# Ten of 31 convolution taps moved to ScalarE, the last block shared anew, means spread by a matrix of 1/D

## What is computed

```python
def conformer_conv_layer(x, norm_pre, w_pw1, b_pw1, w_dw, b_dw, ln_g, ln_b,
                         w_pw2, b_pw2, norm_post):
    h = rms_norm(x, norm_pre)
    p = jnp.einsum('bsd,de->bse', h, w_pw1) + b_pw1
    g = p[..., :D_C] * jax.nn.sigmoid(p[..., D_C:])
    conv = lax.conv_general_dilated(
        g, w_dw[:, None, :], window_strides=(1,), padding=[(CONV_K - 1, 0)],
        dimension_numbers=('NWC', 'WIO', 'NWC'), feature_group_count=D_C) + b_dw
    c = jax.nn.silu(layer_norm(conv, ln_g, ln_b))
    y = jnp.einsum('bse,ed->bsd', c, w_pw2) + b_pw2
    return x + rms_norm(y, norm_post)
```

## Time and profile before

| | before |
|---|---|
| median of 3 runs | 2025.27 us (2024.93 to 2025.52) |
| span of the profiled execution | 2021.2 us |
| TensorE busy | 1998.1 us (99%) |
| weight loads of TensorE busy | 1696.4 us (84%) |
| VectorE busy | 1189.4 us (59%) |
| ScalarE busy | 983.6 us (49%) |
| GpSimd busy | 199.5 us (10%) |

### The profile page before, as it was taken

One profiled execution on the slowest core, in us unless ns is written; L12 is line 12 of the kernel. 1 busy time (PEld: TensorE's weight loads), 2 busy tenths in 40 slices (PEclk: granted clock), 3 DMA queues, 4 the chain that ended last, 5 costly groups with the idle time before them and its releaser, 6 DMA issues.

```text
span 2021.2 us, 27616 instructions
## 1 busy us (share of the span) xinstructions
PE 1998.1 (99%) x9842; PEld 1696.4 (84%) x9842; DVE 1189.4 (59%) x1499; ACT 983.6 (49%) x1150; POOL 199.5 (10%) x123
## 2 busy tenths in 40 slices
PE   9999999999999999999999999999999999999998
PEld 7898888888888888888899977888888888888886
DVE  5755565555555554444799975655555555554444
ACT  6544464545455443433744464454444444443433
POOL 1000000000000000000689830000000000000000
PEclk9999999999999999999999989999999999999999
DMA  9745566766666765555355525566666666665554
GB/s 324 238 144 191 176 217 221 222 216 213 217 216 219 219 219 195 192 196 191 127 189 179 177 94 198 168 238 217 211 215 222 216 222 212 217 212 194 193 192 146
DMA packets 137966, 407.58 MB, mean 202 GB/s; under 512 B 15330, under 2 KB 38498, under 8 KB 137378
## 3 DMA queue, kind: packets, MB, share of 16 engines
q1 hardware_dynamic: 135796, 396.84, 59.6%
q0 software_dynamic: 2096, 9.70, 1.4%
HBM read 392.84 MB, written 13.63 MB: 201 GB/s over the span
## 4 chain that ended last, share of the span: by engine, by line
PE 88%; DVE 9%; ACT 1%; DMA 1%; issue 1%; SPq 0%; POOL 0%; DVEq 0%; ACTq 0%
PE acc L1297 83%; DVE acc L1211 7%; PE acc L1308 1%; PE acc L1310 1%; PE acc L1309 1%; PE acc L1538 1%; DMA raw<-in_units 1%; PE acc L1349 0%; ACT w_hi L570 0%; DVE gated L1198 0%; DVE conv L1216 0%; DVE conv L1211 0%; DVE w_lo L915 0%; DVE conv L1249 0%; PE acc L1347 0%
## 5 line engine op out<-in xcount | busy, mean ns | idle before, releaser
L917 DVE SCALAR_TENSOR_TENSOR w_lo<-raw,vecs,w_hi 128x1024 fp32r<-128x1024 f32 x398 | 509.2, 1282 | 437.3 <-ACT w_hi L570 437.1
L570 ACT ACTIVATE w_hi<-raw,vecs 128x1024 fp32r<-128x1024 f32 x398 | 457.8, 1152 | 514.2 <-PE acc L1297 471.9
L570 ACT ACTIVATE w_hi<-raw 128x1024 fp32r<-128x1024 f32 x304 | 321.2, 1059 | 397.2 <-PE acc L1297 352.3
L915 DVE TENSOR_TENSOR w_lo<-raw,w_hi 128x1024 fp32r<-128x1024 f32 x236 | 288.9, 1225 | 320.8 <-ACT w_hi L570 320.8
L1297 PE MATMUL acc<-w_hi,xT_hi 128*128 128x512 f32 x1528 | 472.0, 390 | 2.2 <-DVE w_lo L917 1.7
L1297 PE MATMUL acc<-w_lo,xT_hi 128*128 128x512 f32 x1528 | 470.5, 389 | 0.0
L1297 PE MATMUL acc<-w_hi,xT_lo 128*128 128x512 f32 x1528 | 470.5, 389 | 0.0
L1297 PEld LDWEIGHTS acc<-w_hi,xT_hi 128*128 128x128 f32 x1528 | 285.7, 188 | 63.7 <-issue 3.4
L1297 PEld LDWEIGHTS acc<-w_hi,xT_lo 128*128 128x128 f32 x1528 | 286.8, 188 | 59.8
L1297 PEld LDWEIGHTS acc<-w_lo,xT_hi 128*128 128x128 f32 x1528 | 286.8, 188 | 59.7
L1297 PE MATMUL acc<-w_lo,hT_hi 128*128 128x512 f32 x704 | 217.4, 389 | 0.0
(11 more groups left out here) (171 smaller groups left out, 1444.3 us busy)
## 6 DMA issues: line engine op xcount, KB each, us to landing
raw<-in_units SPq DMA_DIRECT2D x702, 512.0 KB, 3.8
hid_turned_blocks<-tok SPq DMA_DIRECT2D x44, 256.0 KB, 2.8
tok<-hid_turned_blocks SPq DMA_DIRECT2D x176, 64.0 KB, 2.8
gpost<-in_post POOLq DMA_DIRECT2D x4, 1024.0 KB, 6.0
x<-in_x POOLq DMA_DIRECT2D x4, 512.0 KB, 11.1
c_raw<-in_consts POOLq DMA_DIRECT2D x4, 512.0 KB, 7.3
out<-x SPq DMA_DIRECT2D x8, 256.0 KB, 2.8
xT_raw<-in_xT SPq DMA_DIRECT2D x3, 512.0 KB, 8.9
```

Source lines behind the costliest of these rows:

```text
L570: nc.scalar.activation(w_hi[:, s, :], raw[:, s, :], ACT.Copy, scale=scale).then_inc(hi_ready, 1)
L915: ins = nc.vector.tensor_tensor(w_lo[:, s, :], raw[:, s, :], w_hi[:, s, :], ALU.subtract)
L917: ins = nc.vector.scalar_tensor_tensor(w_lo[:, s, :], raw[:, s, :], vecs[:, gain:gain + 1], w_hi[:, s, :], ALU.mult, ALU.subtract)
```

## The change

- **Taps.** In blocks 0 to 14 ScalarE multiplies taps 21 to 30, two at a time side by side: the first pair into PSUM bank 6, four pairs into SBUF (`prod`). VectorE adds pair after pair 512 wide (`add_tap_pair`), does taps 2 to 20 as before, and adds the two halves of the sum of pairs. The closing add of a block moves behind the first tap of the next, the gate product behind tap 17; that of block 15 stands behind block 14.
- **Block 15.** VectorE takes taps 0 to 18; ScalarE multiplies 19 to 30, TensorE adds these twelve, and VectorE adds the three parts.
- **Means.** A 128 x 128 matrix of 1/D makes mean and spread in one matmul; most of the sums stand ahead of the products of block 15. Only the reciprocal root is still spread by a diagonal. `PE_WARM` goes from 8 to 6.
- **Bias.** Its split moves behind the third quad of the output projection, its memset to GpSimd, both `add_bias` stand inside the projection, each ahead of the fourth quad of its column half.
- **Order of splits.** GpSimd's split of the projection's first quad is interleaved with `add_pair`; ScalarE's last piece of it stands behind the products. The second quad is split two or three steps earlier.

The diff, with indentation cut, continued lines joined and removed lines that the listing above shows cut to the first:

```diff
-PE_WARM = 8
+PE_WARM = 6
+PAIRED = 5
+SINGLE = TAPS - 2 * PAIRED
+LAST_PE = 12
+LAST_DVE = TAPS - LAST_PE
...
-prod = mrow("prod", [P, 4, SEQ])
+prod = mrow("prod", [P, 2 * (PAIRED - 1), SEQ])
-diag = mrow("diag", [P, 2, SEQ])
+pair_sum = mrow("pair_sum", [P, 2 * SEQ])
+diag = mrow("diag", [P, SEQ])
+mean_of = mrow("mean_of", [P, P])
...
+nc.gpsimd.memset(mean_of[:], 1.0 / D).then_inc(consts_set, 1)
...
+split(Q_PW2, 0)
+split(Q_PW2, 1)
 add_pair(PAIRS - 1)
-for s in range(4):
-  split(Q_PW2, s)
+split(Q_PW2, 2)
+split(Q_PW2, 3)
 load_post(2)
+nc.gpsimd.memset(bias_rows[:].bitcast(F32), 0.0).then_inc(bias_cleared, 1)
 inv_root(cvar_ready, 1, crs[:], cvar[:, :, 1], crs_ready)
...
+def tap_pair(n, p):
+  for i in range(2):
+    j = SINGLE + 2 * p + i
+    if p == 0:
+      if n:
+        act.wait_ge(pair_added, (PAIRED - 1) * n)
+      dst = acc[:, 6, i * SEQ:(i + 1) * SEQ]
+    else:
+      if n:
+        act.wait_ge(pair_added, (PAIRED - 1) * (n - 1) + p)
+      dst = prod[:, 2 * (p - 1) + i, :]
+    last = nc.scalar.activation(dst, gated[:, n % RING, j:j + SEQ], ACT.Copy, scale=taps[:, n, j:j + 1])
+  last.then_inc(pair_ready, 1)
 nc.scalar.activation(warm[:], pow_exp[:], ACT.Sigmoid)
-split(Q_PW1 + 1, 0)
...
+for s in range(3):
+  split(Q_PW1 + 1, s)
 for n in range(LAST):
   gate(n)
   split(Q_PW1 + n + 1, 3)
-  if n < INIT_LATE:
-    begin_taps(n)
+  begin_taps(n)
+  tap_pair(n, 0)
   split(Q_PW1 + n + 2, 0)
-  if n >= INIT_LATE:
-    begin_taps(n)
+  tap_pair(n, 1)
+  tap_pair(n, 2)
   split(Q_PW1 + n + 2, 1)
+  tap_pair(n, 3)
+  tap_pair(n, 4)
   if n >= 3 and n % 2:
     square_pair((n - 3) // 2)
+  if n == LAST - 1:
+    square_pair(PAIRS - 1)
   split(Q_PW1 + n + 2, 2)
 gate(LAST)
-split(Q_PW2, 3)
...
 act.wait_ge(conv_ready, LAST)
 nc.scalar.activation(sq_last[:, 0, :], conv[:, LAST - 1, :], ACT.Square).then_inc(sq_last_ready, 1)
-act.wait_ge(prod_used, TAPS)
...
+slots = 2 * (PAIRED - 1)
+act.wait_ge(glu_ready, LAST + 1)
+for i in range(LAST_PE):
+  j = LAST_DVE + i
+  if i >= slots:
+    act.wait_ge(prod_used, i - slots + 1)
+  nc.scalar.activation(prod[:, i % slots, :], gated[:, LAST % RING, j:j + SEQ], ACT.Copy, scale=taps[:, LAST, j:j + 1]).then_inc(prod_ready, 1)
+split(Q_PW2, 3)
 act.wait_ge(conv_last_ready, 1)
 nc.scalar.activation(sq_last[:, 1, :], conv[:, LAST, :], ACT.Square).then_inc(sq_last_ready, 1)
...
-  if k >= KT // 2 and k % 2:
-    split(Q_PW2 + 1, k // 2 - KT // 4)
+  if 5 <= k <= 11 and k % 2:
+    split(Q_PW2 + 1, (k - 5) // 2)
 hi_c(KT - 1)
-for k in range(2, 5):
-  split_quad(Q_PW2 + k)
+split_quad(Q_PW2 + 2)
+split_bias()
+split_quad(Q_PW2 + 3)
+split_quad(Q_PW2 + 4)
...
-nc.vector.memset(bias_rows[:].bitcast(F32), 0.0).then_inc(bias_cleared, 1)
...
-def convolve(n, next_at):
...
+chain_at = {}
+def chain_step(n, half):
+  if (n, half) in chain_at:
+    dve.wait_ge(tap_done, chain_at[n, half])
+  else:
+    dve.wait_ge(taps_begun, 2 * n + 2)
+  chain_at[None] = chain_at.get(None, 0) + 1
+  chain_at[n, half] = chain_at[None]
+  return acc[:, 4 + n % 2, half * SEQ:(half + 1) * SEQ]
+def single_tap(n, j):
+  m = chain_step(n, j % 2)
+  out = conv[:, n, :] if j == SINGLE - 2 else m
+  nc.vector.scalar_tensor_tensor(out, gated[:, n % RING, j:j + SEQ], taps[:, n, j:j + 1], m, ALU.mult, ALU.add).then_inc(tap_done, 1)
+def add_tap_pair(n, p):
+  dve.wait_ge(pair_ready, PAIRED * n + p + 1)
+  if p > 1:
+    dve.wait_ge(pair_added, (PAIRED - 1) * n + p - 1)
+  out = pair_sum[:] if p == PAIRED - 1 else acc[:, 6, :]
+  nc.vector.tensor_tensor(out, acc[:, 6, :], prod[:, 2 * (p - 1):2 * p, :].rearrange("p i n -> p (i n)"), ALU.add).then_inc(pair_added, 1)
+def add_pair_sum(n, half):
+  dve.wait_ge(pair_added, (PAIRED - 1) * (n + 1))
+  m = chain_step(n, half)
+  nc.vector.tensor_tensor(m, m, pair_sum[:, half * SEQ:(half + 1) * SEQ], ALU.add).then_inc(tap_done, 1)
+def close_chain(n):
+  dve.wait_ge(tap_done, chain_at[n, 0])
+  dve.wait_ge(tap_done, chain_at[n, 1])
   nc.vector.tensor_tensor(conv[:, n, :], conv[:, n, :], acc[:, 4 + n % 2, 0:SEQ], ALU.add).then_inc(conv_ready, 1)
+def convolve(n):
+  single_tap(n, 2)
+  if n:
+    close_chain(n - 1)
+  for j in range(3, 13):
+    single_tap(n, j)
+  add_tap_pair(n, 1)
+  single_tap(n, 13)
+  single_tap(n, 14)
+  add_tap_pair(n, 2)
+  single_tap(n, 15)
+  single_tap(n, 16)
+  add_tap_pair(n, 3)
+  single_tap(n, 17)
+  if n < LAST - 1:
+    glu(n + 1)
+  single_tap(n, 18)
+  add_tap_pair(n, 4)
+  single_tap(n, 20)
+  add_pair_sum(n, 1)
+  add_pair_sum(n, 0)
+  single_tap(n, 19)
 glu(0)
 for n in range(LAST):
-  convolve(n, 8 if n == LAST - 1 else 26)
+  convolve(n)
+close_chain(LAST - 1)
+glu(LAST)
+def convolve_last():
+  g = gated[:, LAST % RING, :]
+  half = [acc[:, 5, i * SEQ:(i + 1) * SEQ] for i in range(2)]
+  dve.wait_ge(glu_ready, LAST + 1)
+  nc.vector.tensor_scalar(half[0], g[:, 0:SEQ], taps[:, LAST, 0:1], vecs[:, V_BDW + LAST:V_BDW + LAST + 1], ALU.mult, ALU.add).then_inc(last_tap_done, 1)
+  nc.vector.tensor_scalar(half[1], g[:, 1:1 + SEQ], taps[:, LAST, 1:2], None, ALU.mult).then_inc(last_tap_done, 1)
+  for j in range(2, LAST_DVE):
+    dve.wait_ge(last_tap_done, j - 1)
+    out = conv[:, LAST, :] if j == LAST_DVE - 2 else half[j % 2]
+    nc.vector.scalar_tensor_tensor(out, g[:, j:j + SEQ], taps[:, LAST, j:j + 1], half[j % 2], ALU.mult, ALU.add).then_inc(last_tap_done, 1)
+  dve.wait_ge(prods_summed, 1)
+  dve.wait_ge(last_tap_done, LAST_DVE - 1)
+  after(nc.vector.tensor_tensor(conv[:, LAST, :], conv[:, LAST, :], acc[:, 6, 0:SEQ], ALU.add))
+  dve.wait_ge(last_tap_done, LAST_DVE)
+  nc.vector.tensor_tensor(conv[:, LAST, :], conv[:, LAST, :], half[(LAST_DVE - 1) % 2], ALU.add).then_inc(conv_last_ready, 1)
+convolve_last()
...
-dve.wait_ge(sq_summed, 3)
...
+def centre(k):
+  nc.vector.tensor_tensor(conv[:, k, :], conv[:, k, :], acc[:, 4, 0:SEQ], ALU.subtract).then_inc(c_centred, 1)
+dve.wait_ge(means_ready, 1)
+after(nc.vector.tensor_copy(cvar[:, :, 0], acc[:, 4, SEQ:SEQ + T]))
+after(nc.vector.tensor_tensor(cvar[:, :, 0], cvar[:, :, 0], cvar[:, :, 0], ALU.mult))
+dve.wait_ge(squares_ready, 1)
+after(nc.vector.tensor_tensor(cvar[:, :, 1], acc[:, 7, 0:T], cvar[:, :, 0], ALU.subtract))
 nc.vector.tensor_scalar(cvar[:, :, 1], cvar[:, :, 1], 0.0, EPS, ALU.max, ALU.add).then_inc(cvar_ready, 1)
-for t in range(T):
...
+centre(0)
 dve.wait_ge(crs_ready, 1)
 for t in range(T):
-  last = nc.vector.tensor_scalar(diag[:, 1, t * P:(t + 1) * P], ident[:], crs[:, t:t + 1], None, ALU.mult)
...
+  last = nc.vector.tensor_scalar(diag[:, t * P:(t + 1) * P], ident[:], crs[:, t:t + 1], None, ALU.mult)
+last.then_inc(crs_diag_ready, 1)
 centre(1)
-dve.wait_ge(cst_spread, 2)
+dve.wait_ge(crs_spread, 1)
 for k in range(KT):
   dve.wait_ge(c_centred, k + 1)
-  nc.vector.tensor_tensor(conv[:, k, :], conv[:, k, :], acc[:, 4, 0:SEQ], ALU.mult).then_inc(c_normed, 1)
+  nc.vector.tensor_tensor(conv[:, k, :], conv[:, k, :], acc[:, 6, 0:SEQ], ALU.mult).then_inc(c_normed, 1)
   if k < KT - 2:
     centre(k + 2)
   if k > 1:
     lo_c(k - 2)
-  if k > KT // 2 and k % 2 == 0:
-    split(Q_PW2 + 1, k // 2 - KT // 4 - 1)
+  if 6 <= k <= 12 and k % 2 == 0:
+    split(Q_PW2 + 1, k // 2 - 3)
 lo_c(KT - 2)
 lo_c(KT - 1)
-split(Q_PW2 + 1, 3)
...
+split_quad(Q_PW2 + 2)
+dve.wait_ge(bias_hi_ready, 3)
+nc.vector.tensor_tensor(bias_rows[32:33, :], tok[32:33, :], bias_rows[32:33, :], ALU.subtract).then_inc(bias_lo_ready, 1)
+split_quad(Q_PW2 + 3)
+split_quad(Q_PW2 + 4)
...
-       start=True, stop=False)
+       start=False, stop=False)
...
+def sum_channels(out, src, first, stop):
+  for t in range(T):
+    last = mm(out[:, t:t + 1], src[:, t * P:(t + 1) * P], mean_of[:, 0:1], start=first and t == 0, stop=stop, skip_group_check=True)
   return last
+means, squares = acc[:, 4, SEQ:SEQ + T], acc[:, 7, 0:T]
+def average(src, first, stop):
+  mm(acc[:, 4, 0:SEQ], mean_of[:], src, start=first, stop=stop, skip_group_check=True)
+  return sum_channels(means, src, False, stop)
 pe.wait_ge(consts_set, 4)
 pe.wait_ge(sq_added, 2 * (PAIRS - 1))
 for b in range(2):
-  last = sum_channels(conv_sum[:, b, :], sq_sum[:, b, :], b == 0, False)
-last.then_inc(sq_summed, 1)
+  sum_channels(squares, sq_sum[:, b, :], b == 0, False)
 pe.wait_ge(conv_ready, LAST)
+for b in range(2):
+  average(conv_sum[:, b, :], b == 0, False)
+average(conv[:, LAST - 1, :], False, False)
+for i in range(LAST_PE):
+  pe.wait_ge(prod_ready, i + 1)
+  last = mm(acc[:, 6, 0:SEQ], ident[:], prod[:, i % (2 * (PAIRED - 1)), :], start=i == 0, stop=i == LAST_PE - 1)
+  if i < LAST_PE - 1:
+    last.then_inc(prod_used, 1)
+  else:
+    last.then_inc(prods_summed, 1)
 pe.wait_ge(sq_last_ready, 1)
-sum_channels(conv[:, LAST - 1, :], sq_last[:, 0, :], False, False).then_inc(sq_summed, 1)
+sum_channels(squares, sq_last[:, 0, :], False, False)
 pe.wait_ge(conv_last_ready, 1)
+average(conv[:, LAST, :], False, True).then_inc(means_ready, 1)
 pe.wait_ge(sq_last_ready, 2)
```

(12 more changed lines are left out.)

83 lines of the change are left out of this document (24 added, 59 removed).

## The result

| | before | after |
|---|---|---|
| median | 2025.39 us (2024.93 to 2026.16, 4 runs) | 2011.86 us (2010.40 to 2012.65, 4 runs) |
| span of the profiled execution | 2021.2 us | 2009.8 us |
| TensorE busy | 1998.1 us | 1988.8 us (99%) |
| ScalarE busy | 983.6 us | 1033.4 us (51%) |
| VectorE busy | 1189.4 us | 1182.1 us (59%) |

The ratio is 0.9932 with an interval of 0.9920 to 0.9944. Five more runs of the kernel after (experiment 4) gave 2011.07 (2010.24 to 2014.93). The forecast was 2013.1, range 2009.7 to 2018.

The account below looks back on a forecast made before the run. VectorE's debt of 0.70 us a convolution block, behind full TensorE, ends in a 31.9 us hole before dense work. Earlier start -12.0, split stall -1.3, bias +1.1: -12.2 from 2025.3 gives 2013.1 us, range 2009.7 to 2018.

Parts of the forecast that it names:

- No idle time at 998: First convolution block: moving the bias split removes TensorE's stall on a weight split, 1.57 us from start to start.
- VectorE's block: Convolution stage: VectorE's work per block falls from 12.2 to 11.27 us, 0.25 below TensorE's 11.52.
- rival 1: VectorE, not TensorE, ends the last block, as the clock returns early or never falls: 2011.7 us; chance 0.18.
- rival 2: VectorE still lags: its convolution block is 11.9 us, 0.35 too long, 14 times: 2016.6 us; chance 0.20.
- rival 3: Waits in ScalarE's queue hit the weight splits, TensorE idles 0.8 us a block: about 2025 us; chance 0.05.
- rival 4: VectorE's new adds hold up GpSimd, so TensorE waits 3.1 us a block: 2059 us; chance 0.05.
- the hole: Between the last convolution matmul and the next dense work: 21 to 22 us, where before it was 31.9.
- signs of being wrong: VectorE's block over 11.6; TensorE waiting for GpSimd; GpSimd's root over 0.5 us behind the variance; idle before a bias matmul.
- Term 1: Last block: TensorE's clock falls to half near 1169.3 for 3 to 6.5 us; its summed products are ready at 1180.3.
- Term 2: From last block ready, 1181.2, to dense work, 1188.3: norm steps, with 0.2 for late GpSimd and 0.3 for half clock.
- Term 3: Norm behind the last block: one of two spreads with its diagonal counted as removed from the path.
- Term 4: Whole kernel: -12.2 us, with 4.1 us kept between profiled span and median, gives 2013.1 us.

Follow-up runs that it names:

- experiment 4: Five more runs, on one chip, of the kernel after unchanged, 2011.07 us, and of it with ten matmuls of ones in the idle time, 2007.89 us.
- experiment 5: Kernel after with 8 of the last block's products on TensorE in place of 12, VectorE taking 23 taps: 2010.15 us.
- experiment 2: Kernel after with the bias split, its memset and VectorE's subtraction back in the first block: 2013.61 us.
- experiment 3: Kernel after plus ten matmuls of ones behind TensorE's last convolution matmul: 2007.83 us, ratio 0.9916.
- Experiment 9: Kernel of experiment 3 with the means summed into one column and spread by a diagonal as before: 2008.55 us.
- experiment 7: Kernel of experiment 3 with ScalarE's bias rows and VectorE's memset back in the first block, VectorE's subtraction left late: 2008.50 us.
- experiment 10: Kernel of experiment 3 with ScalarE's and VectorE's splits of the projection's second quad at their old, later places: 2008.68 us.
- experiment 1: Kernel before with only the pairs of taps from the change: 2021.05 us, ratio 0.9980.
- experiment 6: Kernel after with the sum of pairs in SBUF instead of PSUM, so wide adds read two SBUF tiles: 2062.8 us, ratio 1.0187.

## Why the prediction was right, and where its sizes were off

**Right, step by step.** No idle time at 998; last convolution matmul done at 1166.73 where 1166.77 was forecast. VectorE's block 11.31 of work against 11.27, so the lower ends of both bounds were the right ones, as wide adds start 0.60 apart. ScalarE 9.67 against 10.0: four products into SBUF take 1.70 us in its timeline, so they start 0.40 apart and not 0.455, eight times 0.055 less (0.44, of which 0.33 shows). The gate product of block 15 done at 1170.41 against 1170.5. VectorE waits for TensorE's products, as the forecast had it against rival 1, and experiment 5 shows that this wait sets the end. No idle time on a split behind it, and the bias inside the dense work costs its 1.13 us and no waiting (1221.96 to 1223.09 in the trace). Rivals 2, 3 and 4 fall with the profile: no lag, no small idle times, and GpSimd's splits at a median of 2.41 with none above 2.44. Of the signs named, one was missed narrowly: the hole, from the end of the last convolution matmul, was to be 21 to 22 us and was 22.35. None of the signs of being wrong appeared.

**Term 1, too small: the stretch at half clock.** I had products done at 1180.3 from a fall near 1169.3 that lasts 3 to 6.5 us. It came 2.4 us later, at 1171.7, and lasted 6.8, so all of it lay over averages and products: it cost 3.4 us, and they were done at 1181.5. The working itself was loose: a return of the clock at 1172.5 or 1175.7 costs 1.2 or 2.8 us from 1170.1 on, which gives 1179.1 to 1180.7 and not 1179.5 to 1181.1. A second profile of after has 6.9 us, but the same matmuls started 1.4 us later had 10 (experiment 2), and with idle time filled it was mostly nothing. The two falls of the earlier trace rows could not give one number, only a range, from nothing to some 5 us of time: with the idle time filled and no fall the kernel is at 2007.8.

**Term 2, too large: the norm.** From the block ready to dense work I had 7.1 us, of it 0.2 for a late GpSimd and 0.3 for the clock. It was 6.66, so both additions came to nothing. The 0.3 was also counted twice, since the spread already stood at its half-clock length of 0.86; the clock was back at 1178.5. GpSimd's last split, the gain and the memset (1.82 us, near the lower of its bounds) were done 0.8 us before it was needed:

```profile
1181.90 1.82 POOL L556 MEMSET bias_rows<- 64x2048 f32 x1
1184.51 0.72 POOL L471 TENSOR_TENSOR crs<-cvar,pow_exp 128x2 f32<-128x2 f32 x1 [0.79 <-DVE cvar L1329]
```

They were done in time because the block itself came 1.2 us later than forecast; in experiment 3, where it came early, GpSimd went from the memset to the root with no idle time.

**Term 3, wrong in sign: the means.** I counted "one of two spreads with its diagonal" as removed from the path. Experiment 9 shows that it was never worth anything there, and that the matrix costs 0.43 in its place. The three averages ahead of the products, which the forecast had in its sum for TensorE but not in its account of the means, cost 1.3 more where the products set the end.

**Term 4: from span to median.** Sum and span: -12.2 forecast, -11.4 measured. The median moved by 13.5. I had kept 4.1 us between span and median. Every execution's time is its span plus 1.7; the other 2.4 came from the profiled execution of before, which was faster than its median (2021.2 + 1.7 = 2022.9; the runs beside the experiments lie between 2021.8 and 2029.4). So the forecast is 1.2 above the result by two errors that partly cancel: its span of 2009.0 was 0.8 too low, and its distance of 4.1 was 2.0 above the 2011.86 - 2009.8 = 2.1 measured.

Rival 1's 2011.7 is nearer to the result than the forecast's 2013.1. That is no support for it: its mechanism didn't take place in after, and where it nearly did, in experiment 3, the time was 2007.8.

## What to carry to other kernels

When an engine far from full works for the one that sets the pace, look first for the debt at the end of the stage, not for waits inside it: here the 0.7 us a block made no idle time of TensorE inside the stage, and showed only as a gate product 3.51 us late and as part of the 32 us hole. Price a stretch behind idle time or thin matmuls at both clocks and carry the difference as a range; ten matmuls of ones in that gap were worth a quarter as much as the whole change. When work is moved to VectorE beside a busy GpSimd, keep one input in PSUM, and ask of every "removed" step whether it was on the path or inside somebody's wait.

## What the runs showed of the hardware

- A fall of TensorE's clock in the same stretch can differ between kernels that have the same matmuls there, and probably between runs of one kernel. Half clock lasted 6.8 and 6.9 us in two profiles of after, and 10 in that of experiment 2, with the same matmuls. With the ten matmuls of ones in front it lasted 3.4 us in one profile (experiment 7) and did not occur in three (experiments 3, 4 and 10). The medians of after and of the kernel with the ten matmuls differ by 3.2 to 4.0 us, and two runs of the latter lie 3 us above its other three, at a lower mean clock.
- It also came without idle time before it, each time behind a row of one-column sums (experiments 7 and 9, and at 1189.9 in experiment 1). The same sums stood in profiles without a fall.
- A 512-wide add with both inputs in SBUF took 1.91 us instead of 0.69 beside GpSimd's splits, and one such instruction on a single partition, 2.28 us long, lengthened a GpSimd split by 1.13 us (experiments 6 and 7).
- Behind a 512-wide add VectorE's next instruction starts 0.60 us after the add's own start, though the add's record is 0.69 long. The Trainium skill ("VectorE: DVE Perf Modes", the section on the TRN2 errata) gives the length, 691 ns by its formula; the trace agrees with 689, and the overlap comes on top.
